# Where a norm's squares are added up: on VectorE for all nine norms, in place of TensorE for two of them

## The chip, the core and the metric

The kernel runs on one core of a Trainium2 chip. Its engines are TensorE (PE in the profile), VectorE (DVE), ScalarE (ACT), GpSimd (POOL) and SyncE (SP), which here issues DMAs. The metric is the device time of one execution in microseconds (us), smaller is better; runs are compared by their medians.

## What is computed

A transformer-like network of two blocks over 512 tokens of width 1024, with a side stream of 256 context tokens, all in float32. The first block has a chunk MLP with differential attention, a windowed attention and two SwiGLU layers, and ends in a norm. The second has a recurrent stage (HGRN2, 16 heads of 128, both directions) and a last attention with low-rank queries, keys and values (MLA), each with a norm ahead and a norm behind:

```python
def _rmsnorm(x, g):
    xf = x.astype(jnp.float32)
    y = xf * lax.rsqrt(jnp.mean(xf * xf, axis=-1, keepdims=True) + NORM_EPS)
    return (y * g.astype(jnp.float32)).astype(x.dtype)
...
    for i in range(DEPTH):
        h_lat = _rmsnorm(x_lat, norm_pre[i]) * (1.0 + sc_l) + sh_l
        h_ctx = _rmsnorm(x_ctx, norm_pre[i]) * (1.0 + sc_c) + sh_c
...                                     # i = 0: recurrent stage, i = 1: attention
        x_lat = x_lat + gt_l * _rmsnorm(y_lat, norm_post[i])
        if need_ctx:
            x_ctx = x_ctx + gt_c * _rmsnorm(y_ctx, norm_post[i])
```

## The kernel before

Activations lie transposed: x and a are [128 partitions, 8 chunks, 768 tokens], so that a chunk is 128 of the 1024 features (DC = 8) and a token is a column. Tokens 0 to 511 are the latent ones, 512 to 767 the context. Each engine has one program in a fixed order, written out by hand, and the engines wait for each other by counting semaphores. Weights stream through two rings, ringA and ringB; most products are made of three matmuls on rounded high and low parts (L529 and L615).

There are nine norms, numbered 0 to 8 (the list NORMS). A norm needs for each token the sum of squares over all 1024 features, that is over 8 chunks and over the 128 partitions. It goes like this:

- ScalarE squares a chunk (square, L1330), into one of two buffers of sq.
- The squares are summed. In the norms of the list SUMMED, ScalarE writes the square of chunk 0 to rstd instead; VectorE adds the squares of chunks 1 to 6 to it (add_square, L1972, with a drain ahead); TensorE then sums rstd over the partitions with one column of ones (L556) and adds the square of chunk 7 the same way (L560). This takes 6 matmuls each for 768 tokens, and a matmul in float32 is two records in the trace. In the other norms TensorE sums each chunk as it comes (L567), 6 matmuls a chunk and 48 in all, and ScalarE may write the next square but one when a chunk's sum is done.
- VectorE divides by 1024 and takes the reciprocal (L1853, L1855), ScalarE the root (L1362), TensorE spreads it over the partitions by six transposes (L572).
- VectorE scales the chunks (L1887 where a shift follows, L1889 and L1891 else), ScalarE adds the shift (L1381), and where the next product is a split one, VectorE makes the low part (low, L1875).

Norm 5 is the one ahead of the recurrent stage. Norm 4, the final norm of the first block, runs right before it: VectorE scales x in place (L1891), and ScalarE squares the result chunk by chunk. In between VectorE has three weight tiles to split for the recurrent stage (low, L2153), whose high parts come from ScalarE (L1833). While it squares for norm 5, ScalarE also issues the copy of x to memory (x_scratch, L1335), in two halves.

Norm 7 is the one ahead of the last attention. Norm 6, behind the recurrent stage's output product, runs right before it: chunk by chunk, VectorE scales a (L1889) and adds it back to x (add_back, L1881, with a drain ahead), and ScalarE squares the new x for norm 7.

In the kernel before, SUMMED holds norms 0, 1, 2, 3, 4, 6 and 8, so that norms 5 and 7 are the two that TensorE sums by chunk. ADDED and STATS_AT are the counts at which the semaphores sq_added and stat_done stand before and after each norm, and follow from SUMMED.

Of the kernel before, what the change touches and what calls it, by code (L numbers as in the profile page):

```python
# [16 lines left out]
DC = D // P  # L17
# [72 lines left out]
def build(nc, streamA, streamB, streamC, x_in, ctx2_in, smalls_in, consts_in, lvl_in, sgu_in, out):  # L90
    with ExitStack() as ctx:
# [5 lines left out]
        def sem(name):  # L97
            if name not in sems:
                sems[name] = ctx.enter_context(nc.semaphore(name))
            return sems[name]  # L100
# [37 lines left out]
        def SM(name):  # L138
            return smalls[:, SMALL[name][0]:SMALL[name][1]]
# [18 lines left out]
        def flat(ap):  # L158
            return ap.rearrange("p a t -> p (a t)")
# [102 lines left out]
        def pieces(width):  # L262

            return [(0, LAT, 0)] + ([(LAT, CTX, 1)] if width == T else [])


        NORMS = [("norm1_g", 0, "sc1", "sh1", T), ("norm2_g", 0, "sc2", "sh2", T),
                 ("norm1_g", 1, "sc1", "sh1", T), ("norm2_g", 1, "sc2", "sh2", LAT),
                 ("final_g", 0, None, None, LAT),
                 ("norm_pre", 0, "sc", "sh", T), ("norm_post", 0, None, "gt", T),  # L270
                 ("norm_pre", 1, "sc", "sh", T), ("norm_post", 1, None, "gt", LAT)]
# [3 lines left out]
        SPILLS = list(SPILL)  # L275

        FROM_PRODUCT = {1: "even_out", 2: "ffn_out0", 3: "odd_out", 4: "ffn_out1", 6: "hg_out", 8: "mla_out"}
        SUMMED = [0, *FROM_PRODUCT]
        ADDED = {n: (DC - 2) * i for i, n in enumerate(SUMMED)}
        FREE_AT, STATS_AT = {}, {}  # L280
        free_at = stats_at = 0
        for n in range(len(NORMS)):
            if n in FROM_PRODUCT:
                FREE_AT[FROM_PRODUCT[n]] = free_at
                free_at += 4 + DC
            stats_at += 1 if n in SUMMED else DC
            STATS_AT[n] = stats_at
# [38 lines left out]
        def stat_cols(n):  # L326

            return ps[:, 5, 0:NORMS[n][4] // P]

        def rstd_ps(t):  # L330

            return psf[:, 6 * 512 + t.start:6 * 512 + t.stop]
# [173 lines left out]
        def _(pe):  # L506
# [40 lines left out]
            def norm_stats(n):  # L547

                width = NORMS[n][4]
                cols = stat_cols(n)  # L550
                if n in SUMMED:
                    pe.wait_ge(sem("sq_added"), ADDED[n] + DC - 2)
# [753 lines left out]
        def _(act):  # L1306
# [12 lines left out]
            def square(n, c, src):  # L1319

                width = NORMS[n][4]
                if n in SUMMED:
                    dst = rstd[:, 0:width] if c == 0 else sq[:, c % 2, 0:width]
# [521 lines left out]
        def _(dve):  # L1845
            TT, TS, STT = nc.vector.tensor_tensor, nc.vector.tensor_scalar, nc.vector.scalar_tensor_tensor

            def norm(n):
                gains, l, scale, shift, width = NORMS[n]
                gain = SM(gains)[:, 16 * l:16 * l + 16].rearrange("p (c v) -> p c v", v=2) if scale or shift else None  # L1850
                dve.wait_ge(sem("stat_done"), STATS_AT[n])
                nt = width // P
                TS(inv[:, 0:nt], stat_cols(n), 1.0 / D, EPS, ALU.mult, ALU.add)  # L1853
                dve.drain()
                nc.vector.reciprocal(inv[:, 0:nt], inv[:, 0:nt]).then_inc(sem("inv_ready"), 1)  # L1855
                if n == 0:
                    dve.wait_ge(sem("ada_sum"), 4)
                    m, b = ada_places(0, 4, 4)
                    ada_mod(flat(m), flat(b), 2, 0)
                    dve.drain()  # L1860
                if scale:
                    m = MOD[scale, l]
                    STT(coef[:], mod[:, m:m + DC, :], 1.0, gain, ALU.add, ALU.mult)
                elif shift:
                    m = MOD[shift, l]
                    TT(coef[:], mod[:, m:m + DC, :], gain, ALU.mult)
                dve.wait_ge(sem("rstd_spread"), n + 1)
                dve.drain()

                def low(c):  # L1870

                    dve.wait_ge(sem("a_high"), DC * SPLIT.index(n) + c + 1)
                    for t0, tn, v in pieces(width):
                        t, at = slice(t0, t0 + tn), MOD[shift, l] + c
                        last = STT(a_r[:, c, t], a[:, c, t], mod[:, at, v:v + 1], x_r[:, c, t].bitcast(F32), ALU.add, ALU.subtract)  # L1875
                    last.then_inc(sem("a_ready"), 1)

                def add_back(c):

                    dve.drain()  # L1880
                    TT(x[:, c, 0:width], x[:, c, 0:width], a[:, c, 0:width], ALU.add).then_inc(sem("x_ready"), 1)  # L1881

                for c in range(DC):
                    for t0, tn, v in pieces(width):
                        t = slice(t0, t0 + tn)
                        if scale:
                            last = STT(a[:, c, t], x[:, c, t], coef[:, c, v:v + 1], rstd_ps(t), ALU.mult, ALU.mult)  # L1887
                        elif shift:
                            STT(a[:, c, t], a[:, c, t], coef[:, c, v:v + 1], rstd_ps(t), ALU.mult, ALU.mult)  # L1889
                        else:  # L1890
                            last = STT(x[:, c, t], x[:, c, t], SM(gains)[:, c:c + 1], rstd_ps(t), ALU.mult, ALU.mult)  # L1891
                    if scale:
                        last.then_inc(sem("scaled"), 1)
                    elif not shift:
                        last.then_inc(sem("x_ready"), 1)
                    if n in SPLIT and c >= 1:
                        low(c - 1)
                    if n == 6 and c == 0:
                        dve.wait_ge(sem("x_back"), 16 * 6)
                    if not scale and shift:  # L1900
                        add_back(c)
                if n in SPLIT:
                    low(DC - 1)

            def ada_mod(dst, bias, bank, col):

                TT(dst, ps[:, bank, col:col + dst.shape[1]], bias, ALU.add)
# [6 lines left out]
            def ada_places(first, n, c=8):  # L1914

                m = mod[:, c * first:c * (first + n), :].rearrange("p (g c) v -> p g (c v)", c=c)
                b = SM("ada_b")[:, 2 * c * first:2 * c * (first + n)].rearrange("p (g c) -> p g c", c=2 * c)
                return m, b
# [48 lines left out]
            def add_square(n, c):  # L1967

                width = NORMS[n][4]
                dve.wait_ge(sem("sq_ready"), DC * n + c + 1)  # L1970
                dve.drain()
                TT(rstd[:, 0:width], rstd[:, 0:width], sq[:, c % 2, 0:width], ALU.add).then_inc(sem("sq_added"), 1)  # L1972
# [177 lines left out]
            def low(h, s):  # L2150

                dve.wait_ge(sem("hg_high"), h * RB + s + 1)
                TT(ringB_r[:, s, :], ringB[:, s, :], ringA_r[:, s % RH, :].bitcast(F32), ALU.subtract).then_inc(sem("splitB"), 1)  # L2153
# [293 lines left out]
            norm(4)  # L2447
            for s in range(3):
                low(0, s)
            norm(5)  # L2450
            hgrn()
            out_lows("hg_out", 6, lambda k: H["og_low"][:, k, :] if k < DC else H["og"][:, k - DC, :])
# [189 lines left out]
```

## Time and profile before

| | |
|---|---|
| runs | 3675.39, 3671.37, 3667.24 us |
| median | 3671.37 us |
| the profiled execution | 3668.77 us, of which the span of the profile 3666.7 us |
| mean granted clock of TensorE in it | 0.956 of full |
| busy: TensorE, VectorE, ScalarE, GpSimd | 92%, 52%, 32%, 26% of the span |

The profile is of one execution. A row of the timeline gives start and length in us from the span's start, and in brackets how long the engine stood idle before and what released it. The chain is what ended last, followed back step by step. In the rows of stretches, each engine has its busy us and, as x, its instructions; PEclk is the TensorE clock that was granted, as a share of 2.4 GHz; 0.50 is the lower level, 1.2 GHz.

### The profile page before, as it was taken

The page shows a single profiled execution, that of the slowest core. Times are in us where ns is not written, and L with a number is a line of the kernel's source. Part 1 is how long each engine was busy: PE and PEld are TensorE (multiplying, and loading weights), DVE is VectorE, ACT ScalarE, POOL GpSimd, SP SyncE. Part 2 cuts the span into 40 slices and gives each one's busy share as a digit, 9 for nine tenths or more (in the row PEclk, how much of TensorE's full clock was granted, in tenths as well). Part 3 has the DMA queues.
Part 4 walks back from the last instruction along what each step waited for, and adds up shares of the span by engine and source line. Part 5 has one row for each costly group of instructions (what it writes and reads, how often), then busy time and mean ns, then how long its engine had stood idle before and what let it go on. Part 6 is the DMA issues. An engine that isn't in the chain of part 4 may idle for free.

```text
span 3666.7 us, 53931 instructions
## 1 busy us (share of the span) xinstructions
PE 3380.6 (92%) x21376; PEld 2754.8 (75%) x21376; DVE 1889.7 (52%) x2834; ACT 1190.5 (32%) x1843; POOL 961.6 (26%) x436
## 2 busy tenths in 40 slices
PE   6998899999988879999899999999997998999988
PEld 4776788888876657777788888888886784666666
DVE  4455520002346662007657878787878332555556
ACT  3444211112224432112244343433342222444432
POOL 2331435455542045678300000000000520000025
PEclk8999899999989989999899999999997988999989
DMA  6222223333210034444211111111112111111102
GB/s 247 87 75 104 103 92 132 101 134 121 81 64 24 11 117 156 167 164 150 81 53 55 46 55 46 50 47 41 47 35 92 46 46 35 41 40 34 40 29 81
DMA packets 80913, 290.55 MB, mean 79 GB/s; under 512 B 8160, under 2 KB 10208, under 8 KB 79840
## 3 DMA queue, kind: packets, MB, share of 16 engines
q1 hardware_dynamic: 75056, 272.21, 21.9%
q10 hardware_dynamic: 5680, 15.73, 1.1%
q8 instruction: 142, 2.33, 0.3%
q14 instruction: 35, 0.29, 0.0%
HBM read 273.22 MB, written 14.68 MB: 79 GB/s over the span
## 4 chain that ended last, share of the span: by engine, by line
PE 85%; DVE 7%; ACT 3%; DVEq 2%; issue 2%; DMA 1%; ACTq 0%; SPq 0%
PE ps L529 39%; PE ps L615 17%; PE ps L1117 5%; PE ps L514 3%; PE ps L986 2%; PE ps L591 2%; PE ps L837 1%; PE ps L1180 1%; PE ps L567 1%; PE ps L1057 1%; PE ps L1197 1%; PE ps L1047 1%; PE ps L939 1%; DVE ringB_r L2363 1%; ACT arena L1513 1%
## 5 line engine op out<-in xcount | busy, mean ns | idle before, releaser
L466 POOL TENSOR_TENSOR ringB_r<-ringA,consts 128x1024 fp32r<-128x1024 f32 x196 | 394.8, 2014 | 2434.3 <-PE ps L1057 1067.9
L529 PE MATMUL ps<-x_r,ringA_r 128*128 128x512 f32 (+1 forms) x2600 | 734.1, 352 | 23.8 <-ACT arena L1644 13.1
L529 PE MATMUL ps<-x_r,ringB_r 128*128 128x512 f32 (+1 forms) x2600 | 725.6, 349 | 10.8 <-DVE a_r L1875 10.7
L468 POOL TENSOR_TENSOR ringA_r<-ringA,ringB_r 128x1024 fp32r<-128x1024 f32 x196 | 483.8, 2468 | 28.3 <-issue 0.7
L529 PEld LDWEIGHTS ps<-x_r,ringA_r 128*128 128x128 f32 x2600 | 411.3, 189 | 95.2 <-issue 29.3
L529 PEld LDWEIGHTS ps<-x_r,ringB_r 128*128 128x128 f32 x2600 | 412.1, 189 | 86.6 <-issue 20.9
L529 PE MATMUL ps<-a_r,ringA_r 128*128 128x512 f32 x1504 | 388.4, 339 | 8.6 <-issue 8.6
L615 PE MATMUL ps<-a_r,ringB_r 128*128 128x512 f32 (+1 forms) x1440 | 359.9, 358 | 20.5 <-DVE a_r L1925 7.6
L1982 DVE TENSOR_TENSOR arena<-arena,ps 128x768 f32 (+1 forms) x44 | 36.1, 820 | 609.7 <-ACT arena L1397 353.8
L529 PE MATMUL ps<-a_r,ringB_r 128*128 128x512 f32 (+1 forms) x1096 | 330.6, 356 | 0.0
L615 PEld LDWEIGHTS ps<-a_r,ringB_r 128*128 128x128 f32 x1440 | 238.3, 190 | 65.3 <-DVE a_r L1925 16.5
L1925 DVE TENSOR_TENSOR a_r<-arena,a_r 128x768 fp32r<-128x768 f32 (+1 forms) x120 | 193.2, 1653 | 171.9 <-ACT a_r L1409 171.9
L529 PEld LDWEIGHTS ps<-a_r,ringA_r 128*128 128x128 f32 x1504 | 230.1, 188 | 44.1 <-issue 10.5
L615 PE MATMUL ps<-a_r,ringA_r 128*128 128x512 f32 x720 | 217.5, 356 | 0.0
L529 PEld LDWEIGHTS ps<-a_r,ringB_r 128*128 128x128 f32 x1096 | 181.4, 190 | 29.0
L615 PE MATMUL ps<-arena_r,ringB_r 128*128 128x512 f32 (+1 forms) x768 | 193.9, 362 | 8.0 <-DVE arena_r L1925 8.0
L1409 ACT ACTIVATE a_r<-arena 128x768 fp32r<-128x768 f32 (+1 forms) x120 | 82.9, 732 | 282.9 <-PE ps L615 278.4
L1313 ACT ACT_TABLE_LOAD x22 | 28.2, 1283 | 424.6 <-PE ps L591 424.6
L1117 PE MATMUL ps<-arena_r 128*128 128x256 f32 (+1 forms) x768 | 148.1, 319 | 6.0 <-DVE arena_r L2340 3.6
L615 PEld LDWEIGHTS ps<-arena_r,ringB_r 128*128 128x128 f32 x768 | 129.0, 191 | 32.0 <-issue 9.0
L1925 DVE TENSOR_TENSOR arena_r<-arena,arena_r 128x768 fp32r<-128x768 f32 (+1 forms) x64 | 95.3, 1529 | 107.1 <-ACT arena_r L1409 106.9
L514 PE MATMUL ps<-a,ringA 128*128 128x512 f32 (+1 forms) x320 | 143.4, 579 | 0.0
(320 smaller groups left out, 5456.8 us busy)
## 6 DMA issues: line engine op xcount, KB each, us to landing
ringA<-streamA SPq DMA_DIRECT2D x232, 512.0 KB, 3.6
arena<-streamC SPq DMA_DIRECT2D x136, 512.0 KB, 6.6
ringB<-streamB SPq DMA_DIRECT2D x100, 512.0 KB, 3.5
x<-x_in SPq DMA_DIRECT2D x2, 3072.0 KB, 12.5
x_scratch<-x ACTq DMA_DIRECT2D x6, 1024.0 KB, 6.5
a<-streamC SPq DMA_DIRECT2D x8, 512.0 KB, 12.7
x<-x_scratch SPq DMA_DIRECT2D x2, 2048.0 KB, 9.1
x_scratch<-x ACTq DMA_DIRECT2D x2, 1536.0 KB, 7.4
```

The lines of the kernel that those rows point to most:

```text
L466: nc.gpsimd.tensor_tensor(high, ring[:, slot, :], ones[:, 0:1].broadcast_to([P, D]), ALU.mult)
L468: nc.gpsimd.tensor_tensor(ring_r[:, slot, :], ring[:, slot, :], high.bitcast(F32), ALU.subtract) \
L514: mm = nc.tensor.matmul(ps[0:m, bank + half, 0:tn], ring[:, slot, w0 + k * P:w0 + k * P + m], src[:, k0 + k, t0:t0 + tn], start=start and ...
L529: mm = nc.tensor.matmul(ps[:, bank + half, 0:tn], wk, src[:, k, t], start=k == 0 and i == 0, stop=k == DC - 1 and i == 2)
L567: mm = nc.tensor.matmul(cols[:, t:t + 1], sq[:, c % 2, t * P:(t + 1) * P], ones[:, 0:1], start=c == 0 and t == 0, stop=c == DC - 1, skip_g ...
L591: mm = nc.tensor.matmul(ps[32 * j:32 * j + 32, b, at:at + 256], spad[:, vec, 2 * t + k, :], ring[:, t, k, r * 256:(r + 1) * 256], start=t ...
L615: mm = nc.tensor.matmul(ps[:, 2 * n + half, 0:tn], w, src[:, t], start=k == 0 and i == 0, stop=k == nk - 1 and i == 2)
L837: mm = nc.tensor.matmul(ps[:, bank, 0:tn], wk, src[:, c, t], start=c == 0 and i == 0, stop=c == DC - 1 and i == 2)
L986: mm = nc.tensor.matmul(psf[r[0]:r[1], at:at + r[1] - r[0]], H["kl"][:, 2 + p, t], H["ql"][:, p, t], start=True, stop=True)
L1117: mm = nc.tensor.matmul(out, w, src, start=start and i == 0, stop=stop and i == 2, skip_group_check=True)
L1409: nc.scalar.activation(out_ring(name, p, chunk.shape[-1])[0], chunk, ACT.Copy).then_inc(sem("out_high"), 1)
L1925: TT(low, chunk, high.bitcast(F32), ALU.subtract).then_inc(sem("out_low"), 1)
```

## The change

SUMMED becomes all nine norms, so norms 5 and 7 are summed as the others are, and VectorE gets six adds for each. For norm 5 they stand in a row behind the three low parts and ahead of the norm. For norm 7 they stand inside norm 6's loop over the chunks: from chunk 2 on, the square of the chunk before is added right behind the chunk's adding back.

```diff
         FROM_PRODUCT = {1: "even_out", 2: "ffn_out0", 3: "odd_out", 4: "ffn_out1", 6: "hg_out", 8: "mla_out"}
-        SUMMED = [0, *FROM_PRODUCT]
+        SUMMED = list(range(len(NORMS)))
         ADDED = {n: (DC - 2) * i for i, n in enumerate(SUMMED)}
...
                     if not scale and shift:
                         add_back(c)
+                    if n == 6 and c >= 2:
+                        add_square(7, c - 1)
                 if n in SPLIT:
...
             norm(4)
             for s in range(3):
                 low(0, s)
+            for c in range(1, DC - 1):
+                add_square(5, c)
             norm(5)
             hgrn()
```

What this does to the order shows on three engines. Lines of the changed kernel from 1902 on are two higher (L1974 is add_square, L2155 the low part of a weight tile). TensorE, at norm 5, between the transposes of norm 4 and those of norm 5, before (-) and after (+):

```order
 L560 MATMUL ps<-consts,sq 128x1 x4
 L572 MATMUL ps<-consts,st 128x128 x4
-L567 MATMUL ps<-consts,sq 128x1 x48
+L556 MATMUL ps<-consts,rstd 128x1 x6
+L560 MATMUL ps<-consts,sq 128x1 x6
 L572 MATMUL ps<-consts,st 128x128 x6
 L529 MATMUL ps<-x_r,ringA_r 128x512
```

The 48 sums have become 12; at norm 7 it is the same. VectorE at norm 5 in the changed kernel, from norm 4's scaling to norm 5's own:

```order
L1891 SCALAR_TENSOR_TENSOR x<-x,smalls,ps 128x512 x8
L2155 TENSOR_TENSOR ringB_r<-ringB,ringA_r 128x1024 x3
L1974 TENSOR_TENSOR rstd<-rstd,sq 128x768 x6
L1853 TENSOR_SCALAR st<-ps 128x6
L1855 RECIPROCAL st<-st 128x6
```

The six adds are new there; before, L1853 stood right behind the low parts. VectorE in norm 6 before, chunks 2 and 3:

```order
L1889 SCALAR_TENSOR_TENSOR a<-a,coef,ps 128x512
L1889 SCALAR_TENSOR_TENSOR a<-a,coef,ps 128x256
L1881 TENSOR_TENSOR x<-x,a 128x768
L1889 SCALAR_TENSOR_TENSOR a<-a,coef,ps 128x512
L1889 SCALAR_TENSOR_TENSOR a<-a,coef,ps 128x256
L1881 TENSOR_TENSOR x<-x,a 128x768
```

And the same chunks after:

```order
L1889 SCALAR_TENSOR_TENSOR a<-a,coef,ps 128x512
L1889 SCALAR_TENSOR_TENSOR a<-a,coef,ps 128x256
L1881 TENSOR_TENSOR x<-x,a 128x768
L1974 TENSOR_TENSOR rstd<-rstd,sq 128x768
L1889 SCALAR_TENSOR_TENSOR a<-a,coef,ps 128x512
L1889 SCALAR_TENSOR_TENSOR a<-a,coef,ps 128x256
L1881 TENSOR_TENSOR x<-x,a 128x768
L1974 TENSOR_TENSOR rstd<-rstd,sq 128x768
```

An add has come between each chunk's adding back and the next chunk's scaling, so that ScalarE's square of the next chunk waits for one operation more of VectorE. ScalarE has as many squares as before; the first of each norm goes to rstd.

## Rows read from the trace of the kernel before

**Rows 1.** the page: busy times, and the chain that ended last, by engine and line

```profile
PE 3380.6 (92%) x21376; PEld 2754.8 (75%) x21376; DVE 1889.7 (52%) x2834; ACT 1190.5 (32%) x1843; POOL 961.6 (26%) x436
...
PE 85%; DVE 7%; ACT 3%; DVEq 2%; issue 2%; DMA 1%; ACTq 0%; SPq 0%
```

**Rows 2.** the chain of waits around norm 5: start us, us, what

```profile
1799.42 20.65 PE ps L567 x96
...
1820.10 0.17 DVE st L1853
...
1826.15 23.89 PE ps L529 x124
```

**Rows 3.** the chain of waits around norm 7: start us, us, what

```profile
2998.53 0.97 DVE x L1881
...
3000.41 20.65 PE ps L567 x96
...
3021.09 0.16 DVE st L1853
...
3025.91 16.77 PE ps L1096 x32
```

**Rows 4.** timeline of norm 5: start us, us, engine, line, operation [idle before, releaser]

```profile
1798.54 1.56 ACT L1330 ACTIVATE sq<-x 128x768 f32<-128x768 f32 x2
...
1801.20 3.48 DVE L2153 TENSOR_TENSOR ringB_r<-ringB,ringA_r 128x1024 fp32r<-128x1024 f32 x3
...
1815.05 0.37 ACTq L1335 DMA_DIRECT2D x_scratch<-x  x1
1820.10 0.17 DVE L1853 TENSOR_SCALAR st<-ps 128x6 f32<-128x6 f32 x1 [15.41 <-PE ps L567]
```

**Rows 5.** timeline of norms 6 and 7, VectorE and ScalarE

```profile
2997.31 1.14 DVE L1889 SCALAR_TENSOR_TENSOR a<-a,coef,ps 128x512 f32<-128x512 f32 x2 [1.22 <-PE ps L572]
...
3013.11 0.96 DVE L1881 TENSOR_TENSOR x<-x,a 128x768 f32<-128x768 f32 x1
...
3021.09 0.16 DVE L1853 TENSOR_SCALAR st<-ps 128x6 f32<-128x6 f32 x1 [7.02 <-PE ps L567]
```

**Rows 6.** lines by form from 2996 to 3022: xcount | busy us, mean ns | idle before

```profile
L567 PE MATMUL ps<-consts,sq 128*128 128x1 f32 x96 | 20.6, 352 | 3.2 <-ACT sq L1330 3.2
```

**Rows 7.** timeline of norm 0

```profile
23.04 6.21 DVE L1972 TENSOR_TENSOR rstd<-rstd,sq 128x768 f32<-128x768 f32 x6 [16.36 <-ACT sq L1330]
24.03 0.84 ACT L1330 ACTIVATE sq<-x 128x768 f32<-128x768 f32 x1 [0.36 <-DVE rstd L1972]
...
34.81 1.50 PE L556 MATMUL ps<-consts,rstd 128*128 128x1 f32 x12
...
36.17 1.48 PE L560 MATMUL ps<-consts,sq 128*128 128x1 f32 x12
```

**Rows 8.** busy time by engine and granted clock (PEclk) while TensorE sums

```profile
core 0: us, PE busy (x) PEld busy (x) DVE busy (x) ACT busy (x) POOL busy (x), PEclk, DMA share, GB/s
1800.00:1822.00 22.00, 21.24 (x101) 21.11 (x100) 5.09 (x8) 5.37 (x8) 0.00 (x0) 0.50 0.26 96
3000.00:3022.00 22.00, 20.83 (x97) 20.74 (x98) 13.95 (x24) 6.47 (x9) 0.00 (x0) 0.50 0.00 1
```

**Rows 9.** timeline of the stage before norm 5: an add beside GpSimd (POOL)

```profile
1736.12 2.34 POOL L466 TENSOR_TENSOR ringB_r<-ringA,consts 128x1024 fp32r<-128x1024 f32 x1
...
1736.81 2.20 DVE L1972 TENSOR_TENSOR rstd<-rstd,sq 128x512 f32<-128x512 f32 x1
```

**Rows 10.** busy time and granted clock at the restarts, after norms 5 and 7

```profile
1825.00:1828.00 3.00, 1.85 (x6) 1.59 (x7) 3.00 (x6) 1.75 (x4) 0.00 (x0) 0.50 0.01 3
1828.00:1831.00 3.00, 3.00 (x13) 2.62 (x12) 3.00 (x7) 1.33 (x3) 0.00 (x0) 0.66 0.00 0
...
3028.00:3031.00 3.00, 3.00 (x4) 1.09 (x4) 3.00 (x7) 3.00 (x7) 0.00 (x0) 0.50 0.00 0
3031.00:3034.00 3.00, 3.00 (x8) 1.36 (x7) 0.96 (x2) 2.12 (x5) 0.00 (x0) 0.91 0.00 0
```

## The prediction

> **What bounds the kernel now.** First the page's busy shares and its chain of waits [rows 1]: TensorE is busy for 92% of the span and stands for 85% of the chain, so nearly every microsecond by which its work starts later is a microsecond of the total. The two places that the change touches are small in that page, so the rest is read in stretches. In the chain around norm 5 [rows 2], one link is the 96 TensorE records of L567 (48 matmuls, two records each), 20.65 us, and behind it come the reciprocal, the root, the six transposes of L572 and then the first product of the recurrent stage, at 1826.15. The chain around norm 7 [rows 3] has the same link, 20.65 us, and then the first product of the attention stage at 3025.91. So both norms are on the path, and what counts in each is one moment: the start of L1853, which reads the finished sums, at 1820.10 and at 3021.09. What follows it is untouched, and moves with it.
>
> Next, who else works while TensorE sums. In norm 5 VectorE has finished with the three low parts at 1804.68 (1801.20 + 3.48) and then stands idle for 15.4 us [rows 4]. In norm 7 it does not: until 3014.07 it runs norm 6's scaling and adding back without a gap, one chunk every 2.08 us ((3013.11 - 2998.53) / 7), and then waits 7.0 us [rows 5]. The two norms look alike on TensorE and are not alike on VectorE.
>
> **The change part by part.** *Removed:* twice 48 one-column matmuls. A chunk's 12 records take 2.56 us there, a record 0.214 us ((20.65 - 0.35) / 95, with 0.352 for the last to end) [rows 2, 6]. *Added on TensorE:* twice 12 matmuls, 24 records, half from rstd and half from the last square, both after the last add. These forms are seen in norm 0, at full clock, where 12 start in 1.36 us (34.81 to 36.17) [rows 7]. In norms 5 and 7 the granted clock was 0.50, the 1.2 GHz level, for the whole of the old sums [rows 8], and with the change TensorE has had 15 to 23 us without work before its sums. So I take the rate of L567: 23 x 0.214 + 0.35 = 5.27 us; the other end is norm 0's, 24 records in 2.84 us (34.81 to 37.65).
>
> *Norm 5.* VectorE's six adds stand behind the low parts. In norm 0 six adds of this size take 6.21 us from first to last, one every 1.05, and ScalarE's squares keep up, each starting as an add frees its buffer [rows 7]. The first squares are there by 1800.10 (1798.54 + 1.56) [rows 4]. So the adds run from 1804.73 + 0.05 of drain, say 1804.76, to 1810.97. TensorE starts at 1811.00, ends 5.27 later, and L1853 starts at 1816.30 in place of 1820.10: **-3.80 us**. The low parts do not get later, since they stay ahead of the adds. The eighth square, which starts when the fifth add is done, is ready at 1810.8 and hides behind the sixth. The second half of x's spill, issued with that square, goes from 1815.05 [rows 4] to about 1810, so nothing on ScalarE's queue waits longer for it.
>
> *Norm 7.* Here each add goes between one chunk's adding back and the next chunk's scaling, from chunk 2 on. Its square is ready by then (it takes 0.84 us and has a whole chunk's time), so it waits for nothing, but VectorE is full, and what is queued behind each add is the next chunk's scaling, for which ScalarE's square waits, for which the sums wait. A chunk with an add takes 2.08 + 1.05 = 3.13 us. Chunk 7's scaling starts at 2997.31 + 2 x 2.08 + 5 x 3.13 = 3017.12; its adding back starts 1.22 later (2997.31 to 2998.53 [rows 5, 3]), at 3018.34, and ends at 3019.30; the last add runs from 3019.39 to 3020.35. The last square (from 3019.33, 0.84) is ready at 3020.2. TensorE starts at 3020.38 and ends at 3025.65, and L1853 starts at 3025.68 in place of 3021.09: **+4.59 us**. Put otherwise: before, the eight sums started as soon as the first square was there; now six adds of VectorE (6.3 us) and two sums (5.3) stand in the open, and what is saved is only the stretch that TensorE ran behind VectorE's last chunk (3014.07 to 3021.06, 7.0 us).
>
> *Bounds for an add.* Low end 0.96, its own duration [rows 7]. High end 2.20 for two thirds of the elements, in the stage before, where GpSimd was at work in the same microseconds [rows 9]. I take 1.05 for both norms: it is the same form, and GpSimd shows nothing in either stretch [rows 8], as in norm 0.
>
> The Trainium skill, page "VectorE: DVE Perf Modes", section "The DRAIN you can't avoid", says that each VectorE operation is followed by a flush of roughly its duration less 266 ns, and that the next does not start before it; its rules advise few operations. Worked out from that page, an estimate: an add would hold VectorE for 0.96 + 0.69 = 1.65 us, the twelve would cost 7.2 us more than by my 1.05, and the time would be about 3679. The trace goes against it: six adds in 6.21 us [rows 7] leave 0.09 between two.
>
> *Sum.* -3.80 + 4.59 = +0.8 us. Against the profiled execution, 3668.77 (span 3666.70 and 2.07 around it), that is 3669.6. That execution lies 2.6 under the median 3671.37 of the runs shown, so the forecast for the median is **3672.2 us**. The instruction counts elsewhere do not change, and the later stages start from TensorE's first product in each case, so both shifts stay to the end.
>
> **The clock at the restarts.** After each norm the products start at half clock. In norm 5 full clock (2.4 GHz) comes about 3.9 us after the first product (0.66 granted from 1828 to 1831, so full from 1830.0), in norm 7 about 5.6 us after it (0.91 from 3031 to 3034) [rows 10]. A microsecond at half clock costs up to half a microsecond, so the two places already differ by 0.9 us for no reason in the code. With both starts moved, either can fall out the one way or the other: +-0.9 us each, and +-2 for both with the clock drops elsewhere.
>
> **The rivals.**
> - *VectorE hides the adds of norm 7.* Then only the last two steps stand behind chunk 7: adding back ends at 3014.07, an add at 3015.1, sums at 3020.4, L1853 at 3020.4 or 0.6 earlier than now; with norm 5 the total is -4.4, 3667.0. For it: VectorE is busy for only 14.0 of 22 us there [rows 8]. Against: all of that is in the first two thirds, in which it never waits [rows 5].
> - *The new sums run at full clock.* 2.84 in place of 5.27, twice: 0.8 - 4.9 = -4.1, 3667.3. Norm 0 shows such a train at full clock, but right behind products [rows 7]; here nothing runs ahead of it.
> - *Slower: an add holds VectorE for longer than 1.05.* Place: the twelve adds, all of them now on the path. The total passes +7.3 us (0.2%) when an add costs 0.54 more, 1.6 us. With the high end, 2.20 x 768/512 = 3.3 us, it is 12 x 2.25 more: +27.8, 3699. What would cause it is GpSimd at work beside them; it has no work there [rows 8]. The page's 1.65 is just past that point, 3679.
> - *TensorE loses its warmth.* Twenty microseconds of unbroken TensorE work go, and idling takes their place. The Trainium skill, page "TensorE: Matmul & The Clock Gate", section "HAM oscillation — how this bites in real kernels", advises against idle gaps between bursts, since the clock is halved in them. From rows: if the products had started at full clock before and now started at half, that would be half of 3.9 and of 5.6, +4.8 us, 3677. But the clock stood at 0.50 through the removed work and at the restart [rows 8, 10], so that there is nothing to lose but a longer stay there.
>
> **How the numbers follow.** The forecast 0.77 (3672.2, with the clock's +-2: 3670 to 3675); adds hidden 0.04 (3667.0); sums at full clock 0.04 (3667.3); a longer cold restart 0.08 (3677); dear adds 0.07 (3679 and above, mostly just past the point). The runs shown spread from 3667.2 to 3675.4, so a median can lie 2 us off on either side, which is also why 0.2% (7.3 us) is about what can be told from no change. The range takes in all but the dearer adds: 3665 to 3679. Faster by over 0.2% needs under 3664, which no case gives without luck: 0.03. Slower, over 3678.7: the dear adds and the tail of the cold restart, 0.09. Within: 0.88.
>
> **What would show it.** In the chain, the 96-record link of L567 is gone in both places, and L556 and L560 stand there with 24 records. Norm 5: six adds back to back in about 6.2 us right behind the low parts, L1853 some 3.8 us earlier counted from the start of norm 5's first square (now 21.56: 1798.54 to 1820.10; then 17.8). Norm 7: adding back every 3.13 us from chunk 2, and 28.4 us from norm 6's first scaling to L1853 (now 23.78: 2997.31 to 3021.09). The granted clock 0.50 in both sums. Wrong it would be if an add between two chunks cost much less or more than 1.05, if the sums ran at 0.118 us a record, or if the first product's full clock came over 6 us after its start.

## The result, and the profile after

| | before | after |
|---|---|---|
| median of the runs compared | 3671.32 us (7 runs, 3665.13 to 3675.39) | 3657.5 us (7 runs, 3653.43 to 3664.29) |
| ratio, with its 95% interval | | 0.9968 [0.9956, 0.9979] |
| the profiled execution; its span | 3668.77 us; 3666.7 | 3657.3 us; 3655.2 |

The change makes the kernel 13.8 us faster, where the prediction said 0.8 us slower. It lies outside the predicted range.

**The page.** TensorE loses 144 matmul records (21376 to 21232), 72 for each norm, and VectorE gains its twelve adds. The page's counts and its line of shares of the chain answer to [rows 1], and show nothing that would explain 13.8 us:

```profile
PE 3347.8 (92%) x21232; PEld 2722.9 (74%) x21232; DVE 1890.0 (52%) x2846; ACT 1190.3 (33%) x1843; POOL 959.6 (26%) x436
...
PE 84%; DVE 8%; ACT 3%; DVEq 2%; issue 2%; DMA 1%; ACTq 0%; SPq 0%
```

**Norm 5.** The chain around it, start, length in us, what; it answers to [rows 2]:

```profile
1810.35 2.72 PE ps L556 x12
1813.07 2.57 PE ps L560 x12
...
1815.66 0.16 DVE st L1853
...
1821.71 18.47 PE ps L529 x93
```

The link of 96 records is gone. The two sums take 5.3 us together, and L1853 is at 1815.66. The timeline of the same place (start, length, instruction, in brackets the idle time before and what ended it) answers to [rows 4]:

```profile
1798.62 0.83 ACT L1330 ACTIVATE rstd<-x 128x768 f32<-128x768 f32 x1
...
1800.50 3.49 DVE L2155 TENSOR_TENSOR ringB_r<-ringB,ringA_r 128x1024 fp32r<-128x1024 f32 x3
1804.08 6.21 DVE L1974 TENSOR_TENSOR rstd<-rstd,sq 128x768 f32<-128x768 f32 x6
...
1810.35 2.72 PE L556 MATMUL ps<-consts,rstd 128*128 128x1 f32 x12 [15.22 <-DVE rstd L1974]
...
1815.66 0.16 DVE L1853 TENSOR_SCALAR st<-ps 128x6 f32<-128x6 f32 x1 [5.37 <-PE ps L560]
```

The six adds stand behind the low parts and take 6.21 us. From the first square to L1853 it is now 17.04 us.

**Norms 6 and 7.** The timeline again, for [rows 5]: two chunks of norm 6 with the add of norm 7 between adding back and the next scaling, then the last add, the sums and L1853.

```profile
2983.12 1.14 DVE L1889 SCALAR_TENSOR_TENSOR a<-a,coef,ps 128x512 f32<-128x512 f32 x2 [1.22 <-PE ps L572]
...
2988.50 0.96 DVE L1881 TENSOR_TENSOR x<-x,a 128x768 f32<-128x768 f32 x1
...
2989.55 0.96 DVE L1974 TENSOR_TENSOR rstd<-rstd,sq 128x768 f32<-128x768 f32 x1
2990.43 1.13 DVE L1889 SCALAR_TENSOR_TENSOR a<-a,coef,ps 128x512 f32<-128x512 f32 x2
2991.64 0.96 DVE L1881 TENSOR_TENSOR x<-x,a 128x768 f32<-128x768 f32 x1
...
3005.22 0.96 DVE L1974 TENSOR_TENSOR rstd<-rstd,sq 128x768 f32<-128x768 f32 x1
...
3006.23 2.72 PE L556 MATMUL ps<-consts,rstd 128*128 128x1 f32 x12 [23.22 <-DVE rstd L1974]
...
3011.55 0.17 DVE L1853 TENSOR_SCALAR st<-ps 128x6 f32<-128x6 f32 x1 [5.37 <-PE ps L560]
```

A chunk with an add takes 3.14 us (2988.50 to 2991.64). From norm 6's first scaling to L1853 it is 28.43 us. The chain there answers to [rows 3]; no 96-record link is left:

```profile
3006.23 2.72 PE ps L556 x12
3008.95 2.57 PE ps L560 x12
...
3011.55 0.17 DVE st L1853
...
3016.36 16.19 PE ps L1096 x32
```

**The clock.** Stretches of after, with the columns: us, busy time (and instructions) of PE, PEld, DVE, ACT and POOL, granted clock, DMA share, GB/s. The first two are the stretches of the sums, the others the restarts of TensorE in threes of microseconds; they answer to [rows 8] and [rows 10].

```profile
1798.00:1816.00 18.00, 5.28 (x24) 5.19 (x24) 12.00 (x15) 7.13 (x10) 0.00 (x0) 0.50 0.36 136
2984.00:3011.00 27.00, 4.77 (x23) 4.77 (x23) 21.03 (x29) 6.75 (x8) 0.00 (x0) 0.50 0.00 0
1821.00:1824.00 3.00, 2.29 (x7) 2.02 (x8) 3.00 (x7) 1.52 (x3) 0.00 (x0) 0.50 0.00 0
1824.00:1827.00 3.00, 3.00 (x13) 2.52 (x13) 3.00 (x7) 1.20 (x3) 0.00 (x0) 0.64 0.00 0
3016.00:3019.00 3.00, 2.63 (x3) 1.18 (x4) 3.00 (x7) 3.00 (x7) 0.00 (x0) 0.50 0.03 5
3019.00:3022.00 3.00, 3.00 (x6) 1.29 (x5) 3.00 (x7) 3.00 (x6) 0.00 (x0) 0.69 0.00 0
```

**Where the time went.** L1853 runs once in each norm, so its nine starts cut the span of the profiled execution. In us, between its starts:

| from, to | before | after | difference |
|---|---|---|---|
| start to norm 4 | 1794.5 | 1793.8 | -0.7 |
| norm 4 to norm 5 | 25.6 | 21.9 | -3.7 |
| norm 5 to norm 6: the recurrent stage | 1175.5 | 1165.8 | **-9.8** |
| norm 6 to norm 7 | 25.5 | 30.1 | +4.6 |
| norm 7 to norm 8: the last attention | 629.5 | 627.1 | -2.4 |
| norm 8 to the end | 16.1 | 16.5 | +0.4 |

The two rows that the change touches did what was forecast. Most of the gain comes from a stage in which not one instruction is different.

**Inside the recurrent stage.** TensorE runs 14 of the 16 heads there in a hardware loop (L1082), seven rounds of two heads, 1988 of its instructions a round; the last two heads stand behind it. The timeline of TensorE in before, where the loop jumps back to its start (L1068 is the end of a round, L529 the start of the next):

```profile
2000.22 0.82 PE L1068 MATMUL ps<-consts,arena 128*128 128x128 f32 x6
2002.15 0.61 PE L529 MATMUL ps<-x_r,ringA_r 128*128 128x512 f32 x2 [1.11 <-issue]
...
2003.66 0.40 PE L529 MATMUL ps<-a_r,ringA_r 128*128 128x512 f32 x1
2005.48 0.39 PE L529 MATMUL ps<-a_r,ringA_r 128*128 128x256 f32 x1 [1.42 <-issue]
```

TensorE stops twice for "issue", that is, for nothing that the profile shows: for 1.11 us at the first product behind the jump, and again some twenty instruction records further on. The same place in after:

```profile
1995.33 0.82 PE L1068 MATMUL ps<-consts,arena 128*128 128x128 f32 x6
1997.08 0.61 PE L529 MATMUL ps<-x_r,ringA_r 128*128 128x512 f32 x2 [0.94 <-issue]
1997.53 0.51 PE L529 MATMUL ps<-a_r,ringA_r 128*128 128x512 f32 x2
```

The first stop is there, the second is not. In the waits of 1850 to 2760 us (engine, what it was to do, "issue"; us in total, how often, the longest), the stops stand on the weight loads (PEld) and on the matmuls behind them (PE). The two rows overlap in time. Before:

```profile
PEld ps L529 <- issue: 32.1, 26, 2.5
...
PE ps L529 <- issue: 14.6, 12, 2.2
```

After:

```profile
PEld ps L529 <- issue: 22.2, 20, 1.6
...
PE ps L529 <- issue: 6.6, 6, 1.4
```

That is six waits fewer for six jumps back, and 9.9 us less for the weight loads, or 1.65 us each. The stage is 9.8 us shorter.

What the change did to this loop is to move it. Ahead of it in TensorE's program stand 36 matmuls fewer, which are 144 instructions fewer (each matmul is two in the trace, and each of these has a weight load). The instructions themselves are brought by DMA, on a queue of their own, in packets of 16 KB. The DMA view of before, 1900 to 2700 us (packets, MB, share of 16 engines):

```profile
q8 instruction: 64, 1.05, 0.6%
```

The Trainium skill, page "Runtime: NRT & Kernel Launch", section "Instruction fetch mechanics", says that TensorE holds 2048 instructions, refilled in 16 KiB blocks of 256, and that a taken branch whose target is outside the current window of two pages, as it also calls the blocks, has to wait for a fetch. The packets of 16 KB in the trace agree with the block, and the stops behind the jump with the wait.

The trace of before shows this wait at the branch itself. The view of the loop's line gives the duration of its branches in ns (least, median, longest):

```profile
L1082 PEldq COMPARE_BRANCH  x7: 83/3511/3887, 1998.3 to 2738.8; - x7
```

And that of the loop in the last attention, which has 602 instructions:

```profile
L1252 PEldq COMPARE_BRANCH  x7: 76/208/231, 3162.9 to 3495.4; - x7
```

The seventh branch of L1082, which does not jump, takes 0.08 us; the six that jump take 3.37 to 3.89. In each of the six one packet of the instruction queue starts 0.94 to 1.15 us after the branch does and has landed 1.35 to 1.52 us before it ends. The branch is taken up while earlier products still run (at 1998.26, with products up to 2001.04), so only about 1 us of it is seen as a stop. The second stop has a packet too: it starts 0.7 to 1.9 us after the end of the branch and has landed 1.24 to 1.59 us before the stop ends. In after, the second packet comes as well, but no stop stands there.

### The profile page after: what moved, and what is told of

Read it like the earlier page. It is cut to its first block, busy times and chain, and to the rows that moved or that the text cites. A ratio compares the mean times of both kernels' runs of the same rounds, so it can differ in the third digit from the quotient of the medians.

```text
span 3655.2 us, 53665 instructions
## 1 busy us (share of the span) xinstructions
PE 3347.8 (92%) x21232; PEld 2722.9 (74%) x21232; DVE 1890.0 (52%) x2846; ACT 1190.3 (33%) x1843; POOL 959.6 (26%) x436
## 4 chain that ended last, share of the span: by engine, by line
PE 84%; DVE 8%; ACT 3%; DVEq 2%; issue 2%; DMA 1%; ACTq 0%; SPq 0%
PE ps L529 39%; PE ps L615 17%; PE ps L1117 5%; PE ps L514 3%; PE ps L986 2%; PE ps L591 2%; PE ps L837 1%; PE ps L1180 1%; PE ps L1057 1%; PE ps L1047 1%; PE ps L1197 1%; PE ps L939 1%; DVE ringB_r L2365 1%; ACT arena L1513 1%; PE ps L691 1%
## 5 line engine op out<-in xcount | busy, mean ns | idle before, releaser
L529 PE MATMUL ps<-x_r,ringA_r 128*128 128x512 f32 (+1 forms) x2600 | 734.1, 352 | 24.4 <-ACT arena L1644 13.1
L529 PE MATMUL ps<-x_r,ringB_r 128*128 128x512 f32 (+1 forms) x2600 | 724.8, 349 | 11.0 <-DVE a_r L1875 11.0
L529 PEld LDWEIGHTS ps<-x_r,ringA_r 128*128 128x128 f32 x2600 | 411.0, 189 | 95.0 <-issue 29.9
L529 PEld LDWEIGHTS ps<-x_r,ringB_r 128*128 128x128 f32 x2600 | 411.8, 189 | 86.9 <-issue 21.2
L529 PE MATMUL ps<-a_r,ringA_r 128*128 128x512 f32 x1504 | 386.7, 338 | 0.0
L529 PE MATMUL ps<-a_r,ringB_r 128*128 128x512 f32 (+1 forms) x1096 | 330.1, 356 | 0.0
L529 PEld LDWEIGHTS ps<-a_r,ringA_r 128*128 128x128 f32 x1504 | 229.9, 188 | 33.7
L529 PEld LDWEIGHTS ps<-a_r,ringB_r 128*128 128x128 f32 x1096 | 181.0, 189 | 29.0
L1313 ACT ACT_TABLE_LOAD x22 | 28.2, 1283 | 424.5 <-PE ps L591 424.5
```

The lines of the kernel that those rows point to most:

```text
L529: mm = nc.tensor.matmul(ps[:, bank + half, 0:tn], wk, src[:, k, t], start=k == 0 and i == 0, stop=k == DC - 1 and i == 2)
```

## The experiments

Five questions: which half of the change brings the 9.8 us; whether the place of the loop in the program does it, and with which period; where within a block a loop stands best; what it costs to have the loop at all; and how the change stands without that effect. All medians are beside the kernel before on the same chip. The stages of all runs are in a table at the end. Where increments stand at the start of TensorE's program, later lines of the kernel are two higher, so that L531 is the L529 of before.

**e1_norm5_only**: norm 5 as in after, norm 7 as in before.

```diff
-        SUMMED = list(range(len(NORMS)))
+        SUMMED = [n for n in range(len(NORMS)) if n != 7]
...
-                    if n == 6 and c >= 2:
-                        add_square(7, c - 1)
```

> Norm 5 alone gets the six adds and the twelve sums; norm 7 keeps its 48 sums by chunk. Both theories agree that norm 5 itself gives 3.8 to 4.4 us and norm 7 costs nothing here. Theory A (place of TensorE's loop in its instruction stream): the recurrent stage has the same TensorE instructions ahead of it as with the whole change, so that it too is 9.8 us shorter: about 3671 - 4.4 - 9.8 = 3657, less up to 2 us of what the whole change gained behind norm 7, and 4.6 us below the whole change if that gain comes from this half: 3653 to 3657. The stop 19 records behind the loop's jump back (1.2 to 2.6 us in each of six rounds of the loop before) is absent. Theory B (the recurrent stage gained by chance, or from the adds of both norms): 3667.

3656.07 us beside 3670.57, ratio 0.9962 [0.9948, 0.9976]. The recurrent stage takes 1164.5 us, and only the first stop is there. Norm 5's half brings all of the gain: 144 instructions fewer ahead of the loop are enough.

**e2_norm7_only**: the other half.

```diff
-        SUMMED = list(range(len(NORMS)))
+        SUMMED = [n for n in range(len(NORMS)) if n != 5]
...
-            for c in range(1, DC - 1):
-                add_square(5, c)
```

> Norm 7 alone gets the adds; norm 5 keeps its 48 sums by chunk. Theory A: nothing ahead of the recurrent stage has changed in TensorE's stream, so the stage is as long as before, with its second stop in each round of the loop, and the total rises by norm 7's 4.6 us: 3674 to 3676. Theory B: the gain does not hang on norm 5's code, and the total is under 3670.

3674.54 us, ratio 1.0012 [1.0002, 1.0022], which is +4.4 us (+0.7 to +8.1); the medians are 4.0 apart. The recurrent stage is at 1178.3 and both stops are there. Norm 6 to norm 7 takes 30.1 us as in after. So this stage is longer by what the prediction said, +4.59, and the total agrees within its interval.

**e3_after_pad144**: after, with as many instructions put back ahead of norm 5 as the change took out. They add 1 to a semaphore that nobody reads and do no other work.

```diff
             norm_stats(4)
+            for _ in range(144):
+                pe.sem_inc(sem("pad"), 1)
             norm_stats(5)
```

> The whole change, with 144 semaphore increments (one instruction each, 0.051 us in the trace, 7.3 us in all) on TensorE between norm 4's sums and norm 5's, where it stands idle for 15 us. They put the recurrent loop back to where it lay in the stream before the change, and touch nothing else. Theory A: the second stop behind the jump back returns, 1.2 to 2.6 us in each of six rounds, and the time is some 10 us above the whole change: 3665 to 3669. Theory B: as the whole change, 3657.

3674.73 us, ratio 1.0009 [1.0, 1.0019]. Both stops are back, and the recurrent stage takes 1180.1 us. But the filler is dearer than expected, as the timeline shows:

```profile
1803.96 6.21 DVE L1976 TENSOR_TENSOR rstd<-rstd,sq 128x768 f32<-128x768 f32 x6
...
1816.54 2.69 PE L556 MATMUL ps<-consts,rstd 128*128 128x1 f32 x12 [21.54 <-issue]
```

The adds end at 1810.17, and the sums start only at 1816.54, behind 21.54 us that are 144 increments of 0.15 us. So this run is 6.3 us late for a second reason (norm 4 to norm 5 takes 28.2 us for 21.9 in after), its total lies above the 3665 to 3669 that were expected, and e6 repeats it without that.

**e4_before_pad112**: before, with 112 increments at the very start of TensorE's program, where it waits for its first weights. 112 forward is the same place in a block of 256 as 144 back.

```diff
             pe.sem_inc(readB, RB)
+            for _ in range(112):
+                pe.sem_inc(sem("pad"), 1)
```

> The kernel before, with 112 semaphore increments (5.7 us) at the very start of TensorE's program, where it waits 10.7 us for the first weights. All of its later instructions lie 112 further, which in steps of 256 instructions is where the whole change puts the recurrent loop (144 back). Both norms are as before. Theory A: the second stop is gone, and the time falls by some 10 us with no change in the work: 3660 to 3664. Theory B: no change, 3669 to 3673.

3659.28 us beside 3670.57, ratio 0.997 [0.9958, 0.9983]: the kernel before, with 112 instructions more that do nothing, is 11 us faster. In its waits the six are gone, as in after:

```profile
PEld ps L531 <- issue: 21.9, 20, 1.6
...
PE ps L531 <- issue: 6.4, 6, 1.4
```

The recurrent stage takes 1163.3 us. Norm 4 to norm 5 takes 26.4 us and norm 6 to norm 7 25.5 (before: 25.6 and 25.5), so the gain does not come from the norms at all. The increments were not all hidden, since 112 of them take 17 us: the first product starts at 18.47 in place of 10.73. But the next one waits for a transfer in both kernels, and the sums of norm 0 start only 0.5 us later (35.35 for 34.81).

**e5_after_pad72**: after, with 72 increments in the place of e3, which is half of the way back.

```diff
             norm_stats(4)
+            for _ in range(72):
+                pe.sem_inc(sem("pad"), 1)
             norm_stats(5)
```

> The whole change with 72 increments between norm 4's sums and norm 5's (0.151 us apart in the run with 144 of them, so 10.9 us, inside the 15 us in which TensorE stands idle there). Half of the shift that brought the second stop back. Theory A in the form that only a block boundary close behind the jump back costs anything (19 instructions behind it before, some 163 with the whole change, some 91 here): no second stop, 3655 to 3660. If instead the stop grew evenly with the shift: half of it, 3662.

3657.76 us beside 3672.64, ratio 0.9961 [0.9946, 0.9975], only the first stop, recurrent stage 1165.4. With the end of a block some 90 instructions behind the loop's start instead of some 20, there is no second stop.

**e6_after_pad144_hidden**: e3 with the increments where they cost nothing: 64 at the start, 80 ahead of norm 5.

```diff
             pe.sem_inc(readB, RB)
+            for _ in range(64):
+                pe.sem_inc(sem("pad"), 1)
...
             norm_stats(4)
+            for _ in range(80):
+                pe.sem_inc(sem("pad"), 1)
             norm_stats(5)
```

> The whole change with 144 increments again, 64 at the start of TensorE's program (9.7 us of the 10.7 that it waits there) and 80 ahead of norm 5 (12.1 us of 15), so that none of them is in the open, where the run with 144 in one place began norm 5's sums 5.7 us late. Theory A: the second stop is back and nothing else: 10 us above the whole change, 3665 to 3670. If the earlier rise came from the late start and its consequences: 3657 to 3660.

3671.74 us beside 3672.64, ratio 1.0003 [0.9993, 1.0012], 1.7 us above the range expected. The recurrent stage takes 1176.5 us, and both stops are back, to the count:

```profile
PEld ps L531 <- issue: 32.2, 26, 2.6
...
PE ps L531 <- issue: 14.8, 12, 2.3
```

Norm 4 to norm 5 takes 21.9 us here and norm 6 to norm 7 30.1, as in after. This is the kernel that the prediction had in mind: the change, with the loop at its old place in a block. By its ratio it comes out at +1.1 us (-2.6 to +4.4), by the two medians (before 3672.64) at -0.9, where +0.8 was forecast.

**e7_after_pad188**: after, moved by 188 in all (64 at the start, 60 between two products of early rows, 64 ahead of norm 5). The loop then starts near a block's start. 1988 instructions would fit into eight blocks (2048), and if TensorE kept eight, the jump would find its target there.

```diff
             pe.sem_inc(readB, RB)
+            for _ in range(64):
+                pe.sem_inc(sem("pad"), 1)
...
             ada_rows(0, 0, 0)
+            for _ in range(60):
+                pe.sem_inc(sem("pad"), 1)
...
             norm_stats(4)
+            for _ in range(64):
+                pe.sem_inc(sem("pad"), 1)
             norm_stats(5)
```

> The whole change with 188 increments, all hidden (64 at the start, 60 behind the first weights, where TensorE waits 12 us, 64 ahead of norm 5). The recurrent loop has 1988 TensorE instructions, and instruction packets of 16 KB come in all through it, 64 in 800 us, while in the two feed-forward loops (472 and 279 instructions) and the attention's (602) none come. If the second stop marks a boundary of blocks of 256, these increments put the loop's start some 24 instructions behind a boundary, and the loop then touches 8 blocks and not 9. By the Trainium skill, page "Runtime: NRT & Kernel Launch", section "Instruction fetch mechanics", TensorE's instruction memory holds 2048 instructions, 8 blocks. If a loop of 8 blocks stays in it: no instruction packets in the loop and no stop at all behind the jump back, 6 x 1.2 us less than the whole change, 3649 to 3652. If it does not stay: as the whole change, 3655 to 3660.

3656.62 us, ratio 0.9963 [0.9949, 0.9978]. The first stop stays:

```profile
PEld ps L531 <- issue: 21.2, 20, 1.4
...
PE ps L531 <- issue: 5.7, 6, 1.2
```

and the instruction queue still brings the loop in every round, with 59 packets for 64:

```profile
q8 instruction: 59, 0.97, 0.5%
```

So that idea falls. The loop is fetched again each round at each of the four places that the experiments gave it (e5, e7, before and after), and its jump back costs the first stop. In the trace each round of e7 brings nine packets and each round of before ten, one more than the eight and nine blocks that the loop lies in. Whether it is that one more that pushes out the loop's first block was not tried.

**e8_norm5_pad188**: the same 188 in e1, that is, without norm 7's half.

```diff
-        SUMMED = list(range(len(NORMS)))
+        SUMMED = [n for n in range(len(NORMS)) if n != 7]
...
-                    if n == 6 and c >= 2:
-                        add_square(7, c - 1)
```

(and the three pieces of e7)

> The same 188 increments with norm 5 alone changed, norm 7 by chunk as before: the version that should be the fastest. 4.6 us below the run with both norms and 188 increments if norm 7's adds cost what the forecast said: 3645 to 3648 if the loop stays in the instruction memory, 3652 to 3656 if not.

3659.48 us, ratio 0.9955 [0.9938, 0.9972], runs from 3651.33 to 3660.42. The recurrent stage, 1164.6 us, is e7's, and norm 6 to norm 7 takes 25.6, as in e1. The profiled execution was 5.8 us behind e7's at the first product of the recurrent stage already, from stages that are the same in both. The stages say what was expected. The total lies above the 3652 to 3656 expected, and the totals of the two can't be told apart.

**e10_before_unrolled**: before, with TensorE's loop over the heads written out, so that there is no jump back. The same instructions, seven times as many of them in the program.

```diff
-                with pe.Fori(0, HEADS // 2 - 1) as g:
+                for g in range(HEADS // 2 - 1):
```

> The kernel before, with TensorE's loop over the heads of the recurrent stage written out: seven rounds of two heads stand one behind the other in the program, with no jump back. The work, its order and the other engines' programs are the same. If both stops in a round come from the jump back (the first, about 1.2 us and there in every run so far, and the second, 1.2 to 2.9 us, there only with a block boundary close behind the loop's start): 6 x 1.1 + 10 us less than before, 3653 to 3657, and no stop over 0.9 us on a product in that stage. If only the second does, because the first is the wait of the transposes ahead of it: 3660 to 3663.

3651.77 us beside 3672.3, ratio 0.994 [0.9926, 0.9954], 20 us faster, a little more than expected. No wait of L529 for "issue" is left in the stretch. The place where the loop jumped back:

```profile
2007.00 0.82 PE L1068 MATMUL ps<-consts,arena 128*128 128x128 f32 x6
2007.58 0.59 PE L529 MATMUL ps<-x_r,ringA_r 128*128 128x512 f32 x2
2008.01 0.52 PE L529 MATMUL ps<-a_r,ringA_r 128*128 128x512 f32 x2
```

The recurrent stage takes 1157.1 us, 18.4 less than before and 7.4 less than e1. The queue of instructions has less to bring, although the written-out program is longer:

```profile
q8 instruction: 51, 0.84, 0.4%
```

**e9_norm5_unrolled**: e1 with the loop written out.

```diff
-        SUMMED = list(range(len(NORMS)))
+        SUMMED = [n for n in range(len(NORMS)) if n != 7]
...
-                with pe.Fori(0, HEADS // 2 - 1) as g:
+                for g in range(HEADS // 2 - 1):
...
-                    if n == 6 and c >= 2:
-                        add_square(7, c - 1)
```

> Norm 5 alone changed, and the same loop written out. If the jump back is the cause of both stops: 3656 - 6.6 = 3649.5, the fastest of all runs, and below the kernel before with the loop written out by norm 5's own 3.8 to 4.4 us alone, since the 144 instructions that norm 5 sheds shift no loop now. If shedding them did something besides: a difference nearer 14.

3646.91 us, ratio 0.9929 [0.9915, 0.9942]. This is the fastest kernel of the study, 25.4 us below before (3672.3 in the same comparison), where after was 13.8 below. By the medians it is 4.9 us faster than e10, whose runs spread over 14 us (3644.69 to 3658.72), so that the two intervals overlap; norm 4 to norm 5 is 4.3 us shorter. In this loop no place is in play, and the gain fits norm 5's, forecast at 3.80.

**e11_after_unrolled**: after with the loop written out.

```diff
-                with pe.Fori(0, HEADS // 2 - 1) as g:
+                for g in range(HEADS // 2 - 1):
```

> The whole change with the loop written out. Against the run with norm 5 alone it adds norm 7's adds: by the forecast's term 4.6 us slower, 3654; and by the forecast's own sum (+0.8) no different from the kernel before with the loop written out, within 2 us. If norm 7's adds are hidden after all, as fast as norm 5 alone.

3656.56 us, ratio 0.9962 [0.9949, 0.9976]. Against e9, on the same chip, norm 7's half costs 9.7 us here instead of the 4.6 expected, and against e10 the whole change costs 4.8 instead of 0.8. The profiled executions are 8.5 us apart. Norm 6 to norm 7 takes 30.8 us against 25.5, which is 5.3 of it, and 3.2 lie ahead of norm 4, where both kernels have the same instructions. There the second feed-forward took 416.4 us in this execution and 409.5 in e9's, and other stages made up for half of that. TensorE was at half clock for 21.0 us of that stage here and for 11.6 in e9; in the other kernels the stage took 408.9 to 414.7 us, with 7.5 to 18.0 at half clock. So this part is scatter of the clock, as far as one profiled execution of each can tell.

**All stages**, in us between the starts of L1853 (two to six lines further down where increments stand above it), and the profiled execution:

| kernel | stops | norm 4 to 5 | recurrent | norm 6 to 7 | attention | profiled |
|---|---|---|---|---|---|---|
| before | two | 25.6 | 1175.5 | 25.5 | 629.5 | 3668.8 |
| e2_norm7_only | two | 26.5 | 1178.3 | 30.1 | 628.2 | 3672.5 |
| e3_after_pad144 | two | 28.2 | 1180.1 | 30.1 | 626.8 | 3677.6 |
| e6_after_pad144_hidden | two | 21.9 | 1176.5 | 30.1 | 628.9 | 3671.2 |
| after | one | 21.9 | 1165.8 | 30.1 | 627.1 | 3657.3 |
| e1_norm5_only | one | 22.4 | 1164.5 | 25.5 | 629.4 | 3656.9 |
| e4_before_pad112 | one | 26.4 | 1163.3 | 25.5 | 631.1 | 3658.1 |
| e5_after_pad72 | one | 21.9 | 1165.4 | 30.1 | 627.1 | 3657.5 |
| e7_after_pad188 | one | 22.2 | 1164.7 | 30.1 | 626.9 | 3655.5 |
| e8_norm5_pad188 | one | 22.4 | 1164.6 | 25.6 | 630.6 | 3660.4 |
| e10_before_unrolled | none | 26.2 | 1157.1 | 25.5 | 631.2 | 3658.7 |
| e9_norm5_unrolled | none | 21.9 | 1155.6 | 25.5 | 630.9 | 3648.3 |
| e11_after_unrolled | none | 22.4 | 1155.4 | 30.8 | 630.9 | 3656.8 |

Four kernels have two stops and a recurrent stage of 1175.5 to 1180.1 us, six have one and 1163.3 to 1165.8, three have none and 1155.4 to 1157.1. The groups don't touch, and which norms were changed does not matter to them.

## Why the prediction missed

**Norm 5, -3.80: right.** L1853 came 3.7 us earlier counted from norm 4's. The adds took the forecast 6.21 us, the sums 5.3 at half clock. From first square to L1853 it was 17.04 us for the forecast 17.8, because the low parts started 0.7 us earlier (1800.50 for 1801.20 [rows 4]), as norm 4 had, and the first square did not (1798.62 for 1798.54).

**Norm 7, +4.59: right for the stage.** 28.43 us for 28.4, 3.14 a chunk for 3.13. Full VectorE and open adds were the right reading of [rows 5]. In the totals this price is seen less well: by the medians +4.0 (e2 against before), -2.9 (e7 against e8) and +9.7 (e11 against e9), while the stage is 4.6, 4.6 and 5.3 us longer.

**The price of an add, 1.05 us, and the clock, 0.50 in both sums: right.** By an estimate from the Trainium skill's page "VectorE: DVE Perf Modes", section "The DRAIN you can't avoid", a chunk would have been 3.73 us long in place of 3.13; the trace has 3.14. The rival of dear adds falls with that, and so do the adds hidden in norm 7 and the sums at full clock.

**The restarts: within their margin.** The clock reached its full level 4.5 us after the first product in both places (0.64 granted from 1824 to 1827, so full from 1826.2; 0.69 from 3019 to 3022, so full from 3020.9), where the prediction had 3.9 and 5.6 and allowed 0.9 each.

**The step that failed** is the last sentence of the sum: "The instruction counts elsewhere do not change, and the later stages start from TensorE's first product in each case, so both shifts stay to the end". It took the length of the recurrent stage as given, because its work is. Its work was the same; its instructions stood elsewhere relative to the blocks in which they are fetched, and six stops of 1.65 us went (1175.5 us for the stage became 1165.8). This is 9.8 of the 11.5 us that separate the profiled executions. e4 shows it without any change to a norm, and e6 shows the change without it, within 4.4 us of no difference, as predicted. The last attention was taken as given by the same sentence, and was 2.4 us shorter, for a reason that stays open (below).

The rows for it were in the trace of before: the waits for "issue" of the line that carries most of the chain, twelve of them with a longest of 2.2 us, exactly two for each of six jumps. The prediction read the waits around the two norms and none of the stage between. Had it done so, it could not have told which way 144 instructions would push the loop without counting the program's instructions. But it would have had a rival on the fast side, at up to the 14.6 us of those twelve waits, and a wider range.

**What stays open.** The attention stage took 626.8 to 628.9 us in six of the seven kernels with norm 7 changed, and 629.4 to 631.2 in those without; the seventh, e11, has 630.9. The shorter ones spend 50 to 53 us of it at half clock, against 58 to 61. Why the clock does better there was not tried. Nor is it settled why e11 lies 4.8 us above e10.

## What to carry over

Where a hardware loop is fetched again in each round, as the one of 1988 instructions is here, the program's length ahead of it is part of its cost: before an edit that adds or removes instructions is priced, list the waits for "issue" and the durations of the branch in every loop behind it, and count the waits against the loop's rounds. A long loop that stops at each jump back is worth writing out (here 20 us for one line), and a change should be judged with that effect taken out, by a filler that puts the loop back at its old place, since otherwise a lucky place is taken for the worth of the change. For a sum over chunks: adds on an engine that idles are a gain, on one that is full they stand in the open; the best kernel here takes the norm 5 half alone.

## What the runs showed of the hardware that was not expected

- A jump back of TensorE's loop over 1988 instructions costs a stop at the first product behind it, on average 0.9 to 1.1 us on the matmuls (5.4 to 6.6 us for six where it stands alone), at each of the four places tried. With the end of a block some 20 instructions behind the loop's start there is a second stop, on the matmuls of before 1.4 us on average (0.84 to 2.21), on the weight loads 1.65 by the difference to after; with it some 90 or more behind, none (e5, after, e1, e4, e7, e8).
- A branch that jumps back in this loop takes 3.37 to 3.89 us in before, against 0.21 us (the median) in the three shorter loops.
- Moving the program by 112 forward does the same as by 144 back, so the period is 256 instructions or a divisor of it. The written-out program (e10) settles which: 800 us of it are 6.6 rounds of 120.5 us, or some 13200 instructions, in 51 packets, which is some 260 each, and no divisor of 256 but 256 itself is near that. A packet is 16 KB (1.05 MB in 64), which makes 64 bytes an instruction.
- Short loops are not fetched again. The two feed-forward loops of TensorE have 472 and 279 instructions in 11 rounds. In before no packet came over the instruction queue q8 in 520 to 840 us, in the first of them:

```profile
q1 hardware_dynamic: 10433, 37.98, 35.0%
q14 instruction: 1, 0.01, 0.0%
```

The same holds for the second (1430 to 1650 us) and for the loop of the last attention, 602 instructions (3180 to 3480 us). By the page of the Trainium skill named above, TensorE holds 2048 instructions, so that these loops fit; the loop of 1988 would fit too, and it was fetched again in every round all the same (e7). The page's window of two pages, 512 instructions, would not have held the loop of 602, which was kept. In both the measurement decides.
- A semaphore increment that TensorE's queue carries out by itself takes 0.15 us (144 in 21.5 us), not the 0.05 that was expected of it.
